# Last block of a transformer kernel: weight parts split two ahead from the heads to the wide layer, sigmoids in four halves, mixed chunks rounded later

## What is computed

```
u = rms_norm(h) * (1 + scale1) + shift1
q_a, kc, vc, ksl, vsl, kwn, vwn, g_a, q_b, k_b, v_b, m_a, m_b = split(u @ w_in)
y_a = nsa_attention(q_a, compressed k/v, k_slc, v_slc, k_win, v_win, gates) @ w_up_nsa
y_b = stick_breaking_attention(q_b, k_b, v_b) @ w_up_sb
mixed = (sigmoid(m_a) * y_a + sigmoid(m_b) * y_b) @ w_out
h = h + gate1 * mixed
u2 = rms_norm(h) * (1 + scale2) + shift2
h = h + gate2 * (square(relu(u2 @ mlp_w1)) @ mlp_w2)
```

## Time and profile before

| | us |
|---|---|
| median of 3 runs | 2628.95 (2627.65 to 2629.12) |
| the profiled execution, its time | 2627.96 |
| its span in the trace | 2626.2 |
| PE busy | 2501.7 (95%) |
| DVE busy | 1690.2 (64%) |
| ACT busy | 1299.1 (49%) |
| POOL busy | 432.2 (16%) |

### The profile page before, as it was taken

The page is one execution under the profiler, slowest core; times in us unless marked ns, Lnnn a source line. Parts: engine busy times, 40 slices in busy tenths (PEclk is TensorE's granted clock), DMA queues, the critical chain, the costliest instruction groups (busy, mean ns, idle before and its releaser), DMA issues.

```text
span 2626.2 us, 41667 instructions
## 1 busy us (share of the span) xinstructions
PE 2501.7 (95%) x16702; PEld 2281.8 (87%) x16702; DVE 1690.2 (64%) x3116; ACT 1299.1 (49%) x2451; POOL 432.2 (16%) x389
## 2 busy tenths in 40 slices
PE   7799999999999999888999999999999997997999
PEld 7689999999988888765999999998888886877999
DVE  4734899777777777434479977775555544534654
ACT  4234444666544444434444456665444543463543
POOL 4500000388400000000000018860000000001000
PEclk9799999999999999998999999999999997999999
DMA  6103455433487777520245543346555563213342
GB/s 252 45 33 129 157 184 182 161 129 129 160 279 259 257 267 264 220 75 22 97 161 184 181 166 129 130 138 210 194 195 193 197 227 123 97 65 128 140 182 81
DMA packets 93198, 421.81 MB, mean 161 GB/s; under 512 B 10296, under 2 KB 12880, under 8 KB 85072
## 3 DMA queue, kind: packets, MB, share of 16 engines
q1 hardware_dynamic: 93008, 419.16, 46.2%
HBM read 415.96 MB, written 3.16 MB: 160 GB/s over the span
## 4 chain that ended last, share of the span: by engine, by line
PE 90%; ACT 4%; DVE 4%; DMA 1%; issue 1%; POOL 0%; SPq 0%; POOLq 0%; ACTq 0%; DVEq 0%
PE PS L170 89%; ACT mem L181 2%; DVE mem L191 1%; ACT r_sh L181 1%; DVE hT L199 1%; DVE r_sl L191 1%; PE PS L173 0%; DMA mem<-in_ev_in 0%; ACT r_hhi L181 0%; POOL hT L191 0%; DVE mem L205 0%; DMA mem<-in_v 0%; DMA mem<-in_ada 0%; ACT L188 0%; DVE mem L202 0%
## 5 line engine op out<-in xcount | busy, mean ns | idle before, releaser
L191 DVE TENSOR_TENSOR r_sl<-mem,r_sh 128x1024 fp32r<-128x1024 f32 (+3 forms) x742 | 890.3, 1201 | 674.8 <-ACT r_sh L181 673.9
L181 ACT ACTIVATE r_sh<-mem 128x1024 fp32r<-128x1024 f32 (+3 forms) x742 | 764.9, 1033 | 482.0 <-PE PS L170 428.0
L170 PE MATMUL PS<-r_hhi,r_sh 128*128 128x256 f32 x3280 | 839.3, 292 | 37.5 <-ACT r_hhi L181 19.8
L170 PE MATMUL PS<-r_hlo,r_sh 128*128 128x256 f32 (+1 forms) x3152 | 795.8, 289 | 5.5 <-DVE r_hlo L191 2.6
L170 PEld LDWEIGHTS PS<-r_hhi,r_sh 128*128 128x128 f32 x3280 | 641.5, 196 | 46.5 <-issue 38.9
L170 PEld LDWEIGHTS PS<-r_hlo,r_sh 128*128 128x128 f32 (+1 forms) x3152 | 614.3, 195 | 14.5 <-DVE r_hlo L191 6.5
L170 PE MATMUL PS<-r_hhi,r_sl 128*128 128x256 f32 x3280 | 469.6, 286 | 0.3 <-DVE r_sl L191 0.3
L181 ACT ACTIVATE mem<-PS 128x256 f32<-128x256 f32 (+14 forms) x633 | 217.4, 353 | 475.1 <-PE PS L170 466.0
L170 PEld LDWEIGHTS PS<-r_hhi,r_sl 128*128 128x128 f32 x3280 | 431.6, 195 | 0.8 <-DVE r_sl L191 0.5
L196 POOL TENSOR_SCALAR xT<-cst,mem 128x128 f32<-128x128 f32 x256 | 327.6, 1291 | 620.8 <-ACT mem L181 557.0
L170 PE MATMUL PS<-r_sh,r_ch 128*128 128x512 f32 x1024 | 276.5, 391 | 1.3 <-ACT r_sh L181 1.3
(11 more groups left out here) (129 smaller groups left out, 2137.3 us busy)
## 6 DMA issues: line engine op xcount, KB each, us to landing
mem<-in_u SPq DMA_DIRECT2D x256, 512.0 KB, 3.3
mem<-in_v SPq DMA_DIRECT2D x256, 512.0 KB, 3.9
mem<-in_w SPq DMA_DIRECT2D x16, 2048.0 KB, 8.0
mem<-in_ada SPq DMA_DIRECT2D x48, 512.0 KB, 4.5
mem<-in_in SPq DMA_DIRECT2D x9, 2048.0 KB, 7.9
mem<-in_wq SPq DMA_DIRECT2D x8, 2048.0 KB, 7.9
mem<-in_od_in SPq DMA_DIRECT2D x6, 2048.0 KB, 10.1
mem<-in_ev_in SPq DMA_DIRECT2D x5, 2048.0 KB, 10.6
```

Of the source, the lines that this page charges most:

```text
L170: return self.did(self.e and self.e.matmul(out, lhsT, rhs, start=start, stop=stop, skip_group_check=skip))
L181: return self.did(self.e and self.e.activation(out, in_, func, **kw))
L191: return self.did(self.e and self.e.tensor_tensor(out, a, b, op))
```

## The change

- ScalarE and VectorE split every part from the second of `FILL` to the first of W1 two ahead instead of one: the list `NEXT` holds `FILL`, the 16 parts of the up projections, OUT2 and W1[0]. Parts 0 and 1 are split before the loop starts. In a step of `fill_ac` the `hi` of the part two ahead now stands behind the copy; in a step of `fill_ve` the `lo` of the part two ahead is the whole step.
- The chunks of the stick-breaking result are rounded inside the loop, each behind its copy, and their remainders made there.
- The sigmoids are taken in halves of 1024 columns: the first halves of `ma` and `mb` behind the loop, the second halves at parts 1 and 2 of the up projections; the table for logarithm and exponential is loaded behind the last one.
- The rounding of mixed chunk j moves back to the step of UPS[j+1], behind `hi(UPS[j+2])`; the last chunk's stands behind the loop.
- TensorE waits for activation chunks one at a time, in the first part of each projection alone, instead of for all of them.
- In the output projection `hi(OUT2[c+1])` stands before `square(c-2)`, and `lo(OUT2[c+1])` before the residual addition of chunk c-1.

```diff
-    def mm_T(pe, n, out, s, start=True, stop=True, after_norm=None):
+    def mm_T(pe, n, out, s, start=True, stop=True, after_norm=None, after=None):

         h, l = sh(n), sl(n)
         a = parts[n].a
...
         for k in range(a):
             if after_norm is not None:
                 pe.wait_ge("hhi", after_norm, k)
+            elif after:
+                pe.wait_ge(after[0], k)
             pe.matmul(out, h[:, k, :], s[0][:, k, :], start and k == 0, False)
             if after_norm is not None:
                 pe.wait_ge("hloP" if k % 4 == 3 else "hlo", after_norm, k)
+            elif after:
+                pe.wait_ge(after[1], k)
             pe.matmul(out, h[:, k, :], s[1][:, k, :], False, False)
         pe.wait_ge("lo", n)
         for k in range(a):
...
         W1 = [n for p in range(8) for n in cut_T("w1", p)]
         W2 = [cut_T("w2", p, 32) for p in range(8)]
         FILL = NQB + NKB + NVB + NA + NB
+        UPS_N = [n for pair in zip(UPN, UPS) for n in pair]
+        NEXT = FILL + UPS_N + OUT2 + W1[0:1]

         gs1, gs2 = take(8), take(8)
         B = take(8 * 384).rearrange("p (h n) -> p h n", h=8)
...


         def fill_ac(ac):
-            hi(ac, FILL[0])
             for i, n in enumerate(FILL):
-                if i + 1 < len(FILL):
-                    hi(ac, FILL[i + 1])
                 b = 6 + i % 2
                 if not 8 <= i < 11:
                     ac.wait_ge("wdone", n)
...
                     ac.activation(ma[:, i - 12, :], PS[:, b, 0:256], COPY).then_inc("out", n)
                 elif i >= 20:
                     ac.activation(mb[:, i - 20, :], PS[:, b, 0:256], COPY).then_inc("out", n)
+                hi(ac, NEXT[i + 2])
                 yield
             for c in range(4):
                 ac.wait_ge("onsa", c)
...
             head_norm_ac(ac, qaf, 1024, sq, r, (2, 3), "qa", [("out", N0[3])])
             head_norm_ac(ac, kvTf[:, 512:768], 256, sq[:, 1024:1280], r[:, 1024:1280], (4,), "k1", [("out", N1[3])])
             head_norm_ac(ac, kvTf[:, 768:1024], 256, sq[:, 1280:1536], r[:, 1280:1536], (5,), "k2", [("out", N1[3])])
+            hi(ac, FILL[0])
+            hi(ac, FILL[1])
             fill = fill_ac(ac)
             next(fill)
             ac.wait_ge("kc", 0)
...
                 if i == 9:
                     for _ in fill:
                         pass
-                    ac.wait_ge("out", NB[7])
-                    ac.activation(ma_f, ma_f, ACT.Sigmoid).then_inc("sig", 0)
-                    ac.activation(mb_f, mb_f, ACT.Sigmoid).then_inc("sig", 1)
                 if i >= 3 and (i - 3) % 2:
                     c = (i - 3) // 2
                     ac.wait_ge("sb", i - 3)
-                    ac.activation(osb[:, c, :], PS[:, 4 + c % 2, 0:256], COPY).then_inc("osb", c)
-            for c in range(4):
-                ac.wait_ge("osb", c)
-                ac.activation(qar[:, 256 * c:256 * c + 256], osb[:, c, :], COPY).then_inc("oshi", c)
-            both = [n for pair in zip(UPN, UPS) for n in pair]
-            hi(ac, both[0])
-            for i, n in enumerate(both):
-                if i + 1 < 16:
-                    hi(ac, both[i + 1])
-                if i % 2:
-                    j = i // 2
-                    ac.wait_ge("mix", j)
-                    ac.activation(hhiv[:, j, :], hT[:, j, :], COPY).then_inc("mixhi", j)
-            ac.ready(LNEXP)
-            for c, n in enumerate(OUT2):
-                hi(ac, n)
+                    ac.wait_ge(*ac.activation(osb[:, c, :], PS[:, 4 + c % 2, 0:256], COPY).then_inc("osb", c))
+                    ac.activation(qar[:, 256 * c:256 * c + 256], osb[:, c, :], COPY).then_inc("oshi", c)
+
+            def sigmoid(half, of, name):
+                w = slice(1024 * half, 1024 * half + 1024)
+                ac.wait_ge("out", (NA, NB)[name == "sig_b"][4 * half + 3])
+                ac.activation(of[:, w], of[:, w], ACT.Sigmoid).then_inc(name, half)
+
+            def mix_high(j):
+                ac.wait_ge("mix", j)
+                ac.activation(hhiv[:, j, :], hT[:, j, :], COPY).then_inc("mixhi", j)
+
+            sigmoid(0, ma_f, "sig_a")
+            sigmoid(0, mb_f, "sig_b")
+            for i in range(16):
+                hi(ac, NEXT[28 + i + 2])
+                if i == 1:
+                    sigmoid(1, ma_f, "sig_a")
+                elif i == 2:
+                    sigmoid(1, mb_f, "sig_b")
+                    ac.ready(LNEXP)
+                elif i % 2:
+                    mix_high((i - 3) // 2)
+            mix_high(7)
+            for c in range(8):
+                if c:
+                    hi(ac, NEXT[44 + c + 1])
                 if c >= 2:
                     square(ac, 5, c - 2, ma)
             square(ac, 5, 6, ma)
-            hi(ac, W1[0])
             square(ac, 5, 7, ma)
             norm_ac(ac, 5, lambda c: mod[:, 24 + c:25 + c])

...


         def fill_ve(ve):
-            lo(ve, FILL[0])
             for i, n in enumerate(FILL):
-                if i + 1 < len(FILL):
-                    lo(ve, FILL[i + 1])
+                lo(ve, NEXT[i + 2])
                 yield
             for c in range(4):
                 ve.wait_ge("onhi", c)
...
                 d = ve.tensor_copy(B[:, 2 * p:2 * p + 2, 0:256], PS[:, 2 + p, :].rearrange("p (h n) -> p h n", h=2)).then_inc("B", p)
             ve.wait_ge(*d)
             ve.tensor_copy(B[:, :, 256:384], B[:, :, 128:256]).then_inc("B", 4)
+            lo(ve, FILL[0])
+            lo(ve, FILL[1])
             fill = fill_ve(ve)
             ve.wait_ge(*ve.memset(hid, 0.0).then_inc("dveC"))
             for a in range(2):
...
                     c, hk, br = items[i]
                     soft_ve_a(ve, "ns", i, L, sm, B[:, c + 4 * hk, :])
                 next(fill)
+
+            def stick_low(c):
+                ve.wait_ge("oshi", c)
+                ve.tensor_tensor(osr[:, 256 * c:256 * c + 256], osb[:, c, :], qar[:, 256 * c:256 * c + 256].bitcast(F32), SUB).then_inc("oslo", c)
+
             for i in range(11):
                 if i < 8:
                     ve.wait_ge("log1p", i)
                     ve.scalar_tensor_tensor(A1[i % 3], PS[:, i % 4, 0:384], 0.0, A1[i % 3], MAX, ADD).then_inc("softz", i)
                 next(fill, None)
-            for c in range(4):
-                ve.wait_ge("oshi", c)
-                ve.tensor_tensor(osr[:, 256 * c:256 * c + 256], osb[:, c, :], qar[:, 256 * c:256 * c + 256].bitcast(F32), SUB).then_inc("oslo", c)
-            both = [n for pair in zip(UPN, UPS) for n in pair]
-            lo(ve, both[0])
-            for i, n in enumerate(both):
-                if i + 1 < 16:
-                    lo(ve, both[i + 1])
+                if i >= 5 and i % 2:
+                    stick_low(i // 2 - 2)
+            stick_low(3)
+            for i in range(16):
                 j = i // 2
-                ve.wait_ge("sig", i % 2)
-                ve.wait_ge("wdone", n)
+                lo(ve, NEXT[28 + i + 2])
+                ve.wait_ge("wdone", UPS_N[i])
                 if i % 2 == 0:
+                    ve.wait_ge("sig_a", j // 4)
                     ve.tensor_tensor(ma[:, j, :], PS[:, j % 4, 0:256], ma[:, j, :], MUL).then_inc("up_n", j)
                 else:
+                    ve.wait_ge("sig_b", j // 4)
                     ve.tensor_tensor(mb[:, j, :], PS[:, 4 + j % 4, 0:256], mb[:, j, :], MUL).then_inc("up_s", j)
             for c in range(8):
-                lo(ve, OUT2[c])
+                if 1 <= c < 7:
+                    lo(ve, OUT2[c + 1])
                 if c:
                     residual_add(ve, 4, OUT2, c - 1, lambda c: mod[:, 16 + c:17 + c])
             residual_add(ve, 4, OUT2, 7, lambda c: mod[:, 16 + c:17 + c])
...
                     emptied[b] = ("osb", n // 2)
             n3 = chunks(kvr[:, :], 4), chunks(onr[:, :], 4)
             s3 = chunks(qar[:, :], 4), chunks(osr[:, :], 4)
-            for c in range(4):
-                pe.wait_ge("onlo", c)
-                pe.wait_ge("oslo", c)
             for j in range(8):
                 bank_wait(pe, j % 4)
-                mm_T(pe, UPN[j], PS[:, j % 4, 0:256], n3)
+                mm_T(pe, UPN[j], PS[:, j % 4, 0:256], n3, after=None if j else ("onhi", "onlo"))
                 emptied[j % 4] = ("up_n", j)
                 bank_wait(pe, 4 + j % 4)
-                mm_T(pe, UPS[j], PS[:, 4 + j % 4, 0:256], s3)
+                mm_T(pe, UPS[j], PS[:, 4 + j % 4, 0:256], s3, after=None if j else ("oshi", "oslo"))
                 emptied[4 + j % 4] = ("up_s", j)
             for c in range(8):
-                pe.wait_ge("mixhi", c)
-                pe.wait_ge("mixlo", c)
-            for c in range(8):
                 bank_wait(pe, c)
-                mm_T(pe, OUT2[c], PS[:, c, 0:256], (hhiv, hlov))
+                mm_T(pe, OUT2[c], PS[:, c, 0:256], (hhiv, hlov), after=None if c else ("mixhi", "mixlo"))
                 emptied[c] = ("x", 4, c)
                 if c:
```

## The result

The changed kernel takes 2637.97 us (median of 6 runs, 2637.18 to 2639.03), the kernel before 2627.73 (6 runs): 10.2 us more, ratio 1.0039 with a 95% interval of 1.0026 to 1.0052. It is slower by more than 0.2%. The direction and the range were right, the size was 5.2 forecast against 10.2. The profiled execution of the changed kernel took 2638.15, with a span of 2636.4.

A forecast was written before the change was run, and what follows sets the result against it. TensorE's matmuls bound most of the attention loops and the output projection. Compress +8.3, NSA loop +3.8, up projections -14.3, into output projection -2.7, squares +10.1: +5.2 on 2627.96 gives 2633.2 us (2634.2 at the median), range 2625.5 to 2642.

The forecast's parts named there:

- (a) to (c): Compress stretch: TensorE waits for hrep behind lo(2) +2.5, kcn behind lo(3) +3.0, compressed softmax behind lo(8) +2.9; sum +8.3.
- The ring: NSA loop: VectorE bias, ScalarE exponentials, hi, VectorE lo; the eviction enters, each step 5.20 to 5.48; +3.8 in all.
- The up projections: Gaps of 1.85 and 0.75 near their start, seven later gaps gone, end at 2380.6 instead of 2395.04: -14.3.
- The six stops: Output projection: square(c-2) is issued behind hi(OUT2[c+1]), so TensorE stands 1.68 us six times: +10.1, at least 8.2.
- Rival 1: Output projection: the sums find their squares ready, the 10.1 goes: -4.9, 2624.1 us; chance 0.12.
- rival 2: Compress stretch: the three new waits are covered: -3.1, 2625.9 us; chance 0.10.
- rival 4: Up projections: the gaps stay since chunks and weights share ScalarE, 7.4 back: +12.6, 2641.6 us; chance 0.07.
- The mis-sized term: Compress stretch: half clock from the new idle time was priced at nothing, bounds 0 to +3.
- the step into the output projection: OUT2[0] ends 6.3 us after the up projections' end instead of 8.9, held by hi and lo of OUT2[1]: -2.7.
- Rival 3: Output projection: six stops bring half clock to half of the parts, 8 to 10 more: 2643 us; chance 0.13.
- The table load: Start of the up projections: priced at 1.28 us from the trace; the skill's 2.66 would add 2.8 in all.

The follow-up runs named there:

- experiment 6: Changed kernel with VectorE's copies of hrep, kcn and the compressed softmax put before the remainders of parts 2, 3 and 8: 2627.37 us.
- experiment 4: Changed kernel with parts 0 to 7 (compress stretch) split one ahead, two ahead from the NSA loop's first step on: 2626.50 us.
- experiment 1: Changed kernel with square(c-2) before the rounding of part c+1 in ScalarE's program of the output projection: 2628.36 us.
- experiment 2: Changed kernel with the 28 parts between the attention steps split one ahead again, two ahead only from the up projections on: 2623.52 us.
- experiment 7: Changed kernel with the hrep copy alone moved before the remainder of part 2 in VectorE's program: 2634.29 us, one run.
- experiment 8: Changed kernel with kcn alone moved before the remainder of part 3 in VectorE's program: 2633.72 us, one run.
- experiment 11: Changed kernel, still two ahead, with compress copies before remainders, rounding before the loop's copy, squares first, last mixed chunks first, B's first half sigmoid later: 2613.52 us.
- experiment 10: Kernel of experiments 9 with the first half sigmoid of B moved behind the first rounding of the up projections: 2611.51 us.
- experiments 9: Changed kernel with squares first, attention one ahead, and last multiplication and mixed-chunk roundings before splitting OUT2[1]: 2614.57 us, one run.

## Why the prediction was right, and where its size was off

**Right by its own steps.** The three compress waits, (a) to (c), are in the trace and go when VectorE's order alone is turned, with the same work in the same stretch (experiment 6); the 8.3 of waiting that was forecast measures 8.2 (2.4, 2.9 and 2.9). The ring of 5.20 + 0.28 = 5.48 measures 5.46, and experiment 4 shows its loss with an undisturbed start. The prediction called the ring shorter than TensorE's steps, but its own rows make both 5.20 (57.19 / 11), which is why nearly all of the added 0.28 came through. The up projections ended within 0.4 us of the forecast, with gaps of 1.71 and 0.87 for 1.85 and 0.75, although its working is loose there: 2395.04 less 2380.6 is 14.4, the parts that it lists make 13.5, and 13.9 is measured. The six stops in the output projection cost 10.1 in the forecast, 9.6 in experiment 1 and 10.8 in the account. They do not decide the sign alone: without them the kernel is level with the one before (experiment 1), and the attention's splitting two ahead costs more, 14.4 (experiment 2). Rival 1 (the squares do not hold TensorE) falls with these stops, rival 2 (the compress waits are covered) with experiments 2 and 6, rival 4 with the up projections: their gaps went. By the number alone rival 4 was nearer (12.6 more, and 5.2 for the forecast, where 10.2 was measured); only the trace tells them apart. And the forecast of 5.2 lay on the line of what a measurement can tell from no change. That the kernel came out clearly slower is owed in good part to a cost that the sum had put at nothing.

**The mis-sized term is the clock.** The step read: "The new idle time lies mostly where the clock is already low, so I add nothing, with 0 to +3 as bounds". The compress stretch cost 10.4 instead of 8.3, all of the difference being clock. Before, the 32 small matmuls of the compressed logits ran at a clock near the upper level, between two slow phases (3.99 us); the new wait in front of them brought the lower one forward over them: 6.15. In experiments 7 and 8 they take 6.15 at 0.50 and 3.69 at 1.00. Part 1 ran 0.6 longer as well, and part 2 behind them 0.6 shorter (4.70 from 2211.73 to 2216.43, where 5.29 before, from 2202.91 to 2208.20). The average of 0.83 over the stretch hid that its parts differ. Two windows of 3 us in the trace of the kernel before, which the prediction did not read, show it:

```profile
2199.00:2202.00 3.00, 3.00 (x30) 0.91 0.02 5
2202.00:2205.00 3.00, 3.00 (x15) 0.50 0.78 213
```

Most of the small matmuls lie in the first of them. The same kind of error stands in the step into the output projection, where OUT2[0] was priced at full clock: -1.6 instead of -2.7. Its three stops (1.26, 0.75, 0.42) lie within 3.2 us. Everything up to the last of them came as forecast, but the nine matmuls behind it take 2.3 us instead of 1.3. The windows read:

```profile
2400.00:2403.00 3.00, 2.58 (x12) 0.50 0.98 421
2403.00:2406.00 3.00, 3.00 (x23) 0.93 0.56 240
```

The slow phase reaches into OUT2[1], which takes 3.4 us (2402.58 to 2406.00) where 2.9 before (2403.74 to 2406.61); that is most of what the account has above the 10.1 of the squares. So the sum is: 5.2 forecast, 2.1 of clock in the compress stretch, 1.1 in OUT2[0], 0.7 more in the row of the squares, 0.7 of difference before the stretch, which is not of the change (the eleven variants start it between 2179.4 and 2181.6), and 0.4 from the loop (-0.5), the up projections (+0.4) and the end (+0.5). That makes the 10.2.

**Rival 3, half clock in the output projection, did not come.** From 2402.8 to 2436.3 the clock is 0.99, although TensorE stops for 1.5 in every 5 us. The Trainium skill (TensorE: Matmul & The Clock Gate, A second HAM failure mode: psum-queue depth-cycling) says that frequent small idles between groups of matmuls made the clock swing in one kernel; behind these six, one in every 5.0 us, it did not.

**The table load.** In the changed kernel it starts at 2370.37, right behind a rounding that ends at 2370.35, and the first sigmoid starts at 2371.66, 1.29 later, and the wait of TensorE behind it, 1.71, is under the 1.85 that this price gave. The Trainium skill (ScalarE: Activation LUTs, What ACT_TABLE_LOAD costs) adds a drain of about 1.4 to each switch; the trace does not show it here.

## What to carry to other kernels

On an engine that works in program order, "earlier" means "in front of something": before moving a piece forward, list what then stands behind its wait, and whether another engine waits for that. The change gained where TensorE starved, at the up projections (13.9 us), and lost where TensorE was full or where small dependent steps run between the large ones. Which part of it made the gain is not shown: the halved sigmoids, the rounding inside the loop, the later rounding of the mixed chunks and the splitting two ahead were never tried apart. A few lines of order, squares before roundings and short copies before remainders, turned a loss of 10 us into a gain: 14 with everything two ahead (experiment 11), 16 with the attention one ahead again (experiment 10). And price a new wait in front of small matmuls at both levels of the clock, read from windows of a few microseconds and not from the mean of a stage.

## What the runs showed of the hardware that was not expected

- 32 matmuls of 15 columns take 3.69 us at a granted clock of 1.00 (experiment 8) and 6.15 at 0.50 (experiment 7), though each moves only 15 columns.
- Six stops of 1.5 us, 5.0 us apart, left the clock at 0.99. Stops of 1.26, 0.75 and 0.42 us within 3.2 us went with a fall to 0.50, behind them or among them, in each of the nine traces with this order. Stops of 1.00 and 0.42 were followed by one in experiments 9 and 11 and by none in experiment 10, with the same order of work there. So the stops alone do not decide it; what does is not shown.
- One remainder of a mixed chunk on POOL took 1.57 us at 2396.95 where its neighbours took 0.72 and 0.95; VectorE was busy with a 1.22 us remainder at 2396.71. In experiments 9 and 10, where VectorE's remainder begins 0.6 before POOL's instead of 0.24, it took 1.21 and 1.20. That the one lengthens the other is likely from this, but was not tried by itself.
